# A two-block transformer kernel on one core: the first output projection's groups 0 to 2 computed by token and turned through DRAM

## What is computed

```python
def pool_mixer(h, w_in, w_grp, scale, w_out):
    u, g = jnp.split(h @ w_in, 2, axis=-1)
    ...
    y = jnp.einsum('btgc,gcd->btgd', pooled, w_grp).reshape(B, T, BRANCH_W) * scale
    return (y * jax.nn.silu(g)) @ w_out

x = x + gate * y
return rms_norm(x) * final_norm_g          # end of the first block

hn = rms_norm_2(h, norm_w[i])              # stage A begins
proj = hn @ w_in                           # q, k, v, z and two small columns
```

## Time and profile before

| | |
|---|---|
| Time, median of 3 runs | 1332.98 us (1332.78 to 1334.07) |
| Profiled execution, its own time | 1334.82 us |
| Span of that execution | 1332.7 us |
| PE busy | 99% of the span |
| PEld (weight load) busy | 83% |
| DVE busy | 72% |
| ACT busy | 55% |
| POOL busy | 15% |
| Granted TensorE clock | full in all 40 slices |

### The profile page before, as it was taken

One profiled execution on the slowest core, in us unless ns is written; L12 is line 12 of the kernel. 1 busy time (PEld: TensorE's weight loads), 2 busy tenths in 40 slices (PEclk: granted clock), 3 DMA queues, 4 the chain that ended last, 5 costly groups with the idle time before them and its releaser, 6 DMA issues.

```text
span 1332.7 us, 18992 instructions
## 1 busy us (share of the span) xinstructions
PE 1326.0 (99%) x6963; PEld 1109.1 (83%) x6963; DVE 960.7 (72%) x1279; ACT 732.5 (55%) x1091; POOL 196.8 (15%) x313
## 2 busy tenths in 40 slices
PE   9999999999999999999999999999999999999999
PEld 5445999988888888888888988888888888888887
DVE  4558999988779898999676668746666566666552
ACT  2213435456766657556688775465655646565431
POOL 0000012100001000032122200002234234232000
PEclk9999999999999999999999999999999999999999
DMA  9999989885676776599866676656879889789662
GB/s 383 394 416 371 353 345 408 299 279 181 202 248 207 239 226 222 182 294 293 222 181 198 201 236 224 194 186 205 260 236 270 261 271 283 217 278 262 179 197 83
DMA packets 90354, 339.36 MB, mean 255 GB/s; under 512 B 12368, under 2 KB 12768, under 8 KB 85792
## 3 DMA queue, kind: packets, MB, share of 16 engines
q1 hardware_dynamic: 67392, 261.30, 57.7%
q0 software_dynamic: 22880, 76.94, 19.0%
HBM read 310.91 MB, written 29.38 MB: 255 GB/s over the span
## 4 chain that ended last, share of the span: by engine, by line
PE 81%; DMA 12%; DVE 5%; issue 1%; ACT 1%; SPq 0%; POOL 0%; DVEq 0%; POOLq 0%
PE acc L905 19%; PE acc L848 14%; PE acc L849 14%; PE acc L850 14%; PE acc L909 10%; DMA mod_ring<-mod_w 7%; DMA raw<-weights 5%; PE misc L1174 2%; DVE w_lo L1903 1%; PE misc L905 1%; PE misc L1164 1%; DVE mod_ring L1873 1%; PE misc L1065 1%; DVE mod_late L1873 1%; DVE gate_ring L1873 1%
## 5 line engine op out<-in xcount | busy, mean ns | idle before, releaser
L1903 DVE TENSOR_TENSOR w_lo<-raw,w_hi 128x1024 fp32r<-128x1024 f32 x392 | 471.5, 1221 | 178.7 <-ACT w_hi L1339 173.1
L1339 ACT ACTIVATE w_hi<-raw 128x1024 fp32r<-128x1024 f32 x392 | 405.4, 1054 | 321.6 <-DMA raw<-weights 234.7
L848 PE MATMUL acc<-w_hi,b_op 128*128 128x512 f32 x704 | 277.1, 394 | 0.0
L849 PE MATMUL acc<-w_lo,b_op 128*128 128x512 f32 x704 | 274.3, 390 | 0.0
L850 PE MATMUL acc<-w_hi,b_op 128*128 128x512 f32 x704 | 274.3, 390 | 0.0
L905 PE MATMUL acc<-b_op,w_hi 128*128 128x512 f32 x640 | 162.1, 395 | 0.0
L850 PEld LDWEIGHTS acc<-w_hi,b_op 128*128 128x128 f32 x704 | 132.2, 188 | 27.5
L848 PEld LDWEIGHTS acc<-w_hi,b_op 128*128 128x128 f32 x704 | 132.4, 188 | 26.3
L849 PEld LDWEIGHTS acc<-w_lo,b_op 128*128 128x128 f32 x704 | 132.4, 188 | 26.1
L905 PEld LDWEIGHTS acc<-b_op,w_hi 128*128 128x128 f32 x640 | 115.2, 189 | 21.0 <-issue 0.2
L905 PE MATMUL acc<-a_op,w_hi 128*128 128x512 f32 x448 | 113.1, 394 | 0.3 <-DVE a_op L1913 0.3
(11 more groups left out here) (314 smaller groups left out, 2012.8 us busy)
## 6 DMA issues: line engine op xcount, KB each, us to landing
raw<-weights SPq DMA_DIRECT2D x392, 512.0 KB, 5.1
mod_ring<-mod_w SPq DMA_DIRECT2D x26, 1024.0 KB, 14.4
u_ring<-weights SPq DMA_DIRECT2D x32, 512.0 KB, 14.6
gate_ring<-weights POOLq DMA_DIRECT2D x30, 512.0 KB, 8.3
mod_late<-mod_w SPq DMA_DIRECT2D x6, 1024.0 KB, 6.4
head_d<-head POOLq DMA_DIRECT2D x32, 128.0 KB, 4.3
t<-head_d POOLq DMA_DIRECT2D x32, 128.0 KB, 5.9
z_d<-z POOLq DMA_DIRECT2D x28, 128.0 KB, 4.8
```

The source lines that it names most:

```text
L848: nc.tensor.matmul(to, xh[:, t], wh, start=kt == 0, stop=False)
L849: nc.tensor.matmul(to, xh[:, t], wl, start=False, stop=False)
L1339: nc.scalar.activation(w_hi[:, m.c % HL_SLOTS], raw[:, q.c % RAW_SLOTS], ACT.Copy).then_inc(own.up(s_hi), 1)
L1903: nc.vector.tensor_tensor(w_lo[:, slot], raw[:, q.c % RAW_SLOTS], w_hi[:, slot].bitcast(F32), ALU.subtract).then_inc(own.up(s_lo), 1)
```

## The change

Groups 0 to 2 go by token; ScalarE takes each out of PSUM at its end into a tile in `vo` (`y_part`, two places in turn: tiles 8 to 11, 4 to 7, 8 to 11), VectorE transposes it in blocks into `y_32`, POOL sends it through DRAM and back, and `gated(j)` then adds it onto `xres` from SBUF. Group 3 stays joined. `early_sums` goes from behind the seventh slab of group 3 to behind the fourth of stage A's first group, `last_sums` from behind its fifth to behind its sixth. The weight stream's host layout follows. The core of the diff (left out: the tables of turns, the layout on the host, and helpers that only moved):

```diff
-            for j in range(4):
-                joined(G_WOUT + j, a_op, ready=None if j else lambda kt: O_H + kt // 4 + 1,
-                       fillers={6: early_sums} if j == 3 else None, order=PLAIN if j else SPLIT)
+            for j in range(3):
+                pe.wait_ge(s_free, j + 1)
+                group(None, slab_of(Num(G_WOUT + j)), pair_of_banks(j), 0, a_hi, a_lo, products=by_token,
+                      ready=None if j else lambda kt: O_H + kt // 4 + 1)
+            joined(G_WOUT + 3, a_op)
...
-            joined(G_A, b_op, ready=operand_b, fillers={4: last_sums, 6: decay_and_beta}, order=SPLIT)
+            joined(G_A, b_op, ready=operand_b, fillers={3: early_sums, 5: last_sums, 6: decay_and_beta}, order=SPLIT)
...
+            def out_turned(j):
+
+                n, through = turn_of("y", j), head_d[0] if j == 1 else z_d
+                pool.wait_ge(s_head_32, n)
+                to_dram(y_32[:], through, s_head_d)
+                if j == 0:
+                    for k in (2, 3):
+                        pool.wait_ge(s_gate, 29 + k)
+                        x_again(k)
+                pool.wait_ge(s_head_d, 64 * n)
+                from_dram(through, y_part[j], s_z_t)
...
+            def out_by_token(j):
+
+                act.wait_ge(s_used, slab_of(Num(G_WOUT + j + 1)).c)
+                if j == 2:
+                    act.wait_ge(s_x1, 1)
+                to = y_part[j].rearrange("p (m a c) -> p a m c", m=GM, a=2)
+                src = acc[:, j] if j < 2 else misc[:, 0:2 * GC]
+                for half in range(2):
+                    of = src[:, half * GC:(half + 1) * GC].rearrange("p (m c) -> p m c", m=GM)
+                    nc.scalar.activation(to[:, half], of, ACT.Copy).then_inc(own.up(s_zs if half else s_act), 1)
...
+            def out_turned(j):
+
+                n = turn_of("y", j)
+                dve.wait_ge(s_zs, n)
+                for _ in range(2):
+                    dve.sem_inc(own.also(s_free), 1)
+                if j:
+                    dve.wait_ge(s_head_d, 64 * (n - 1))
+                nc.vector.transpose(y_32[:], y_part[j]).then_inc(own.up(s_head_32), 1)
+
+            def gated(j):
+
+                dve.wait_ge(s_z_t, 64 * turn_of("y", j))
+                dve.wait_ge(s_x_again[j], 16)
+                for m in range(GM):
+                    kt = 4 * j + m
+                    nc.vector.scalar_tensor_tensor(
+                        out=xres[:, kt], in0=tiles(y_part[j])[:, m], scalar=modv[:, 2 * KT + kt:2 * KT + kt + 1],
+                        in1=xres[:, kt], op0=ALU.mult, op1=ALU.add
+                            ).then_inc(own.up(s_x1 if m == GM - 1 else s_dve), 1)
...
             for j in range(4):
-                gated_half(j, 1)
+                if j == 3:
+                    gated_half(3, 1)
+                else:
+                    gated(j)
+                    if j < 2:
+                        out_turned(j + 1)
+                        lo_parts(slab_of(Num(G_WOUT + j)) + (AHEAD + 7), 1)
+                    dve.wait_ge(s_x1, j + 1)
...
-                if j < 3:
-                    lo_parts(n, 4)
-                    gated_half(j + 1, 0)
-                    lo_parts(n + 4, 4)
+                if j < 2:
+                    lo_parts(n + SLABS, SLABS - 1 if j == 0 else 4)
+                    if j == 1:
+                        gated_half(3, 0)
+                        lo_parts(n + 12, 2)
+                elif j == 2:
+                    lo_parts(n + 6, 2)
```

More of the change, by code:

```diff
@@ L153 @@
            ("q", 3), ("k", 3), ("v", 2), ("z", 2), ("v", 3), ("z", 3))
-TURNS = tuple([("va", v) for v in range(4)] + [("za", 0), ("za", 1), ("za", 2)] +
+TURNS = tuple([("y", j) for j in range(3)] + [("va", v) for v in range(4)] + [("za", 0), ("za", 1), ("za", 2)] +
               [of for of in B_ORDER if of[0] in "qk" or of in (("z", 0), ("z", 1), ("z", 2))])
@@ L344, in program @@
         yc = at("yc", [P, 32, 32], F32, a_at + 24576)
+        y_part = [vo[:, k:k + 4].rearrange("p k t -> p (k t)") for k in (8, 4, 8)]
+        y_32 = at("y_32", [P, 4 * T], F32, vo_at + 12288)
         z_32 = [at(f"z_32_{j}", [P, 4 * T], F32, (a_at, vo_at, vo_at)[j]) for j in range(3)]
@@ L649, in _, with to_dram, from_dram @@
                         x_again(j)
-            for j in (2, 3):
-                pool.wait_ge(s_gate, 29 + j)
-                x_again(j)
+            def to_dram(tile, through, written):
+                for a in range(4):
+                    rows = tile[32 * a:32 * a + 32].rearrange("p (n c) -> p n c", c=P)
+                    pool.dma_start(through[:, :, a], rows).then_inc(written, 16)
+            def from_dram(through, tile, done):
+                for b in range(4):
+                    of = through.rearrange("x n a c -> x (n a) c")[:, :, 32 * b:32 * b + 32]
+                    pool.dma_start(tile[32 * b:32 * b + 32].rearrange("p (k t) -> p k t", t=32), of
+                                   ).then_inc(done, 16)
+            def out_turned(j):
[8 more added lines that the diff above has]
+                from_dram(through, y_part[j], s_z_t)
+            out_turned(0)
             pool.dma_start(head_rows[:], rows_d.to_broadcast([P, 2 * P])).then_inc(s_rows, 16)
@@ L655, in _ @@
             pool.dma_start(ab_raw[:], w_ab_d.rearrange("p k c -> p (k c)")).then_inc(s_ab, 16)
+            out_turned(1)
+            out_turned(2)
             def sums_in_rows(i):
@@ L704, in _ @@
                 query_parts(j)
-            def to_dram(tile, through, written):
-                for a in range(4):
-                    rows = tile[32 * a:32 * a + 32].rearrange("p (n c) -> p n c", c=P)
-                    pool.dma_start(through[:, :, a], rows).then_inc(written, 16)
-            def from_dram(through, tile, done):
-                for b in range(4):
-                    of = through.rearrange("x n a c -> x (n a) c")[:, :, 32 * b:32 * b + 32]
-                    pool.dma_start(tile[32 * b:32 * b + 32].rearrange("p (k t) -> p k t", t=32), of
-                                   ).then_inc(done, 16)
             def first_gate_turned(j):
@@ L896, in joined @@
                     if part == 0:
-                        pe.wait_ge(s_free, u - U_WOUT + 1 if g < G_WOUT + 3 else u - 1)
-                    tiles = [(part * SLAB_J + kk, sums_of(u)[:, m * GC:(m + 1) * GC],
+                        pe.wait_ge(s_free, U_WOUT + 2 * (h + 1) if g == G_WOUT + 3 else u - 1)
+                    tiles = [(part * SLAB_J + kk, acc[:, u % 2, m * GC:(m + 1) * GC],
                               slice(kk * HALF + m * P, kk * HALF + (m + 1) * P))
@@ L1449, in _ @@
                 hi_parts(Num(N_GRP + 10 + 2 * j), 1)
-            hi_parts(Num(N_WOUT + 9), 6)
+            def out_by_token(j):
[7 more added lines that the diff above has]
+                    nc.scalar.activation(to[:, half], of, ACT.Copy).then_inc(own.up(s_zs if half else s_act), 1)
+            hi_parts(Num(N_WOUT + 9), 3)
+            out_by_token(0)
+            hi_parts(Num(N_WOUT + 12), 3 + SLABS - 1)
             for j in range(4):
+                if j < 2:
+                    out_by_token(j + 1)
+                    hi_parts(slab_of(Num(G_WOUT + j)) + (AHEAD + 7), 1)
                 if j == 2:
@@ L1480, in _ @@
                     hi_parts(n + 7, 1)
+                elif j == 2:
+                    hi_parts(n + 7, 1)
                 else:
-                    hi_parts(n, SLABS)
+                    hi_parts(n + SLABS, SLABS - 1)
             act.wait_ge(s_ab_mm, 1)
@@ L2080, in gated_half @@
                         nc.vector.scalar_tensor_tensor(
-                            out=xres[:, kt], in0=sums_of(u)[:, (2 * m + part) * T:(2 * m + part + 1) * T],
+                            out=xres[:, kt], in0=acc[:, u % 2, (2 * m + part) * T:(2 * m + part + 1) * T],
                             scalar=modv[:, 2 * KT + kt:2 * KT + kt + 1], in1=xres[:, kt], op0=ALU.mult, op1=ALU.add
@@ L2684, in build_stream @@
         b.append(joined_slabs(m, column) if (kind, j) == ("z", 3) else slabs(m, [column]))
-    rest = np.concatenate([g, grp, joined_stage(i["pool_w_out"][0], quarters), joined_stage(a, order_a[:8]),
+    rest = np.concatenate([g, grp, slabs(i["pool_w_out"][0], quarters[:3]),
+                           joined_slabs(i["pool_w_out"][0], quarters[3]), joined_stage(a, order_a[:8]),
                            *[slabs(a, [c]) for c in order_a[8:15]], joined_slabs(a, order_a[15]),
```

19 lines of the change are left out of this document (9 added, 10 removed).

## The result

The changed kernel takes **1344.97 us** (median of 5 runs, 1342.85 to 1347.61), the kernel before 1333.98 on the same chip: a ratio of 1.0081, 95% interval 1.0064 to 1.0099. It is slower by about 11 us, where 1332.5 was predicted and 1335.9 was the range's end. The profiled execution is the fastest of its runs, 1342.85.

What follows compares the result with a forecast made beforehand. TensorE, 99% busy, was taken as the bound. Terms -0.54 - 1.76 + 0.45 + 1.15 = -0.7 us, with 0.2 for a slightly slow turn, gave -0.5: 1332.5 us, range 1331.2 to 1335.9.

Steps and rivals of the forecast that it cites:

- The pace of TensorE: First output projection: by-token slabs take 2.72 us, saving 1.76 over 24, plus a 0.54 wait; group 2 ends 2.30 earlier.
- Edits that cost nothing: ScalarE's evictions, VectorE's transposes and POOL's 24 DMA issues lie beside slabs prepared up to 7 ahead: put at 0.
- (a) The second pair of banks: Stage A's fourth slab: group 3's banks free at 343.4, just in time for 343.56; wait 0 to 3.65 us, 0.2 taken.
- I take the early end: Group 2's turn, expected between 328.8 and 333.4, taken at 328.8 because DMA engines were 0.41 busy in 316 to 330.
- the late end: Latest arrival of group 2's turned data, 333.4, from the longest turn seen whole.
- the turn is late: Rival, chance 0.26: group 2's turn comes after 329.75, TensorE waits for banks at stage A's fourth slab; up to 3.65, 1335.9 us.
- no term below is one of the clock: Whole kernel: the granted clock is full throughout, so no term was given to it.
- (b): Group 3's squares at `last_sums`, wanted by 352.80: fold ends at 353.55, so the second sum waits about 0.45 us.
- (c): First pair of banks for slab 80: eviction ends at 364.43, TensorE comes 1.1 us ahead and waits; 1.15 in the sum.
- Small pieces: Way back's 128 B pieces, where the skill asks 512 B or more; the trace showed no such price at low load.

Runs made afterwards that it cites:

- few_bytes: Changed kernel, every turn DMA out and back still issued but moving 1 partition's rows in place of 32: 1333.54 us, ratio 0.9997.
- traffic_alone: Kernel before, all four groups joined, with the same twelve DMAs out and twelve back added, their data unused: 1343.34 us, ratio 1.0074.
- no_wait: Changed kernel with whole traffic, but the way back lands in an unread tile and `gated(j)` waits for no turn: 1344.88 us, ratio 1.0074.
- spread_alone: Changed kernel, way out of 1 partition a DMA, way back whole but read from x and spread over 128 partitions: 1338.17 us, ratio 1.0026.
- out_twice: Changed kernel with the way back replaced by a second way out, SBUF to another DRAM tensor, at its place: 1338.72 us.
- dram_back: Changed kernel with the way back replaced by four DRAM-to-DRAM DMAs of 128 KB: 1337.66 us.
- back_few: Changed kernel, each DMA of the way back moving 1 partition's rows in place of 32, the way out whole: 1333.60 us, ratio 0.9996.
- rest_late: Changed kernel with the `head_rows` and `ab_raw` loads issued behind turn 1 in place of turn 0: 1343.79 us, ratio 1.0067.
- one_turned: Changed kernel with only group 0 by token and turned, groups 1 to 3 joined as before: 1340.77 us, ratio 1.0053.
- spread_turn: Changed kernel with a working turn, out in 128 B pieces, back in four DMAs of 1 KB pieces over 128 partitions: 1336.21 us, ratio 1.0020.
- spread_back: Changed kernel, the way back's same bytes in four DMAs over all 128 partitions, 1 KB pieces, not the turned group: 1339.03 us.

## Why the prediction was wrong

- **The pace of TensorE**: right. Group 3 ended at 334.19, predicted 334.19 on this execution's origin, and group 0 met no wait.
- **"Edits that cost nothing"**: this is the step that failed. It counted engines' work and said that it would "lie beside slabs that are prepared up to 7 ahead". It named POOL's 24 DMAs by their issue time and by what stands behind them on POOL, and never priced their 3 MB against the weight stream that feeds both engines. few_bytes shows that this term, put at 0, is 11 us with what follows from it; traffic_alone has 9 us of it on the kernel before.
- **"(a) The second pair of banks"**: the chain was right link by link (10.32 us from the rounding to `gated_half(3, 1)`; in few_bytes the fourth slab is 0.25 late, where just in time was predicted). Its start was wrong: "Slab 77's high part ... waits for slab 69". It waited for its own load and started 8.1 us later (336.88, predicted 328.80 here).
- **"I take the early end"** for the turn, by the load of 0.41 in 316 to 330: the window was that of before, and only turn 2's. The turn's own megabyte was named beside it but added to nothing, and the delayed weights were not thought of. In the changed kernel 320 to 341 is at 0.77 and the way back landed after 7.4 us. The last turn was there at 336.6, beyond the late end (332.4 here).
- **The rival "the turn is late"** had the right symptom, a wait for the banks at the fourth slab, and the wrong cause and size: no_wait takes the turned group off the chain and gains nothing. Its bound of 3.65 us came from the turn's length, while the loss goes by the stream's lateness.
- **"no term below is one of the clock"**: that was read from a trace in which TensorE's longest wait is 1.5 us (0.3 from 240 to 380). Behind the wait of 7.7 us there is such a term, 1.8 us; in traffic_alone it stands behind waits of 2.0 and 1.7.
- **(b) and (c)**: right in size. In few_bytes `last_sums` takes 1.44 us (from 351.88) where it takes 1.03 without a wait, 0.41 more (predicted 0.45), and slab 80's wait is 1.03 (predicted 1.15). In the changed kernel they are 0 and 1.44. With the bytes taken out the whole sum holds: few_bytes is 0.6 us under the kernel before, forecast 0.5.
- **Small pieces**: the doubt that the prediction raised about the 128 B pieces was the wrong feature of the way back. It was the 32 partitions.

What stays open: why 512 KB a turn at the way back's place cost some 4 us even spread or sent out (spread_alone, out_twice, dram_back), where as many at the way out's place cost nothing (back_few). The place is later and beside the re-read of x, `head_rows` and `ab_raw`; no run moves the turn away from these, and rest_late, which moves two of them, is inconclusive. Open too is why two turns' worth of lateness does not add (one_turned 6.4, three turns 11); that the first meets the fullest stretch is argued, not shown.

## What to carry to other kernels

A transfer added beside a stream that feeds the bottleneck is work on that stream's path: price its bytes against the DMA share of every stretch it falls in, before asking who waits for it. With four slots for loads, DMAs that nobody waits for cost 9 us here (traffic_alone). The busy share alone does not say how much: back_few, at 0.97 and 0.91 in the first two stretches, cost nothing. So test it, with the same DMAs moving few bytes. Land transfers on all 128 partitions; if a shuffle needs small pieces, put them on the way out to DRAM.

## What was not expected of the hardware

- Landing 512 KB in DMAs of 32 partitions, or of 64 neighbouring ones, cost 10 us over three turns; over 128 partitions 4 (2.3 in spread_turn, ways out and back together); the way out from 32 partitions nothing at its own place, and 4.3 at the way back's (out_twice).
- Pieces of 128 B against 4 KB made no difference that shows (1344.97 and 1343.22; way back landing 7.4 and 6.6 us), nor did they on the way out (spread_turn 1336.21, spread_back 1339.03).
- After 7.7 us without work TensorE was granted 0.50 of its clock for about 4 us, and the fourth slab took 4.72 us. A wait of 2.0 us was followed by half clock too (traffic_alone, a slab of 4.45 us), and one of 2.6 us was not (spread_turn, 2.90 us, as in few_bytes).
